# A hybrid decoder step on one core: the first two weight groups in four column pieces, and a new order in the head and ahead of the output projection

## The reference, cut to what matters

```python
def rmsnorm(x, g):
    y = xf * lax.rsqrt(jnp.mean(xf * xf, axis=-1, keepdims=True) + EPS)
    return (y * g).astype(x.dtype)
...
(gq, gk, gv, glr, gg, pv, pg, fq, fk, fv, ff, fg) = jnp.split(rmsnorm(h, pre) @ wi, SPLIT_IDX, axis=-1)
g = log_sigmoid(glr @ w_up + b_gate) / GLA_GATE_NORM     # GLA's gates, from 16 columns of wi
logf = log_sigmoid(ff + bf)                              # FoX's gates, from 6 columns of wi
...
y = jnp.concatenate([o_gla * silu(gg), o_pool * silu(pg), o_fox * silu(fg)], axis=-1) @ wo
return h + rmsnorm(y, post)
```

## Time and profile before

| | us |
|---|---|
| median of 3 runs | 697.47 (697.28 to 698.56) |
| the profiled execution | 697.7 |
| its span, first to last instruction | 696.1 |
| PE busy in it | 654.0 (94%) |
| DVE, ACT, POOL busy | 392.2, 261.3, 139.9 |

### The profile page before, as it was taken

How to read it: one execution, slowest core, us unless ns; L and a number is a source line. 1 busy time by engine, 2 the same in 40 slices (tenths; PEclk the granted TensorE clock), 3 DMA queues, 4 the chain that set the end, 5 groups by cost and what they waited for, 6 DMA issues and landing times.

```text
span 696.1 us, 13072 instructions
## 1 busy us (share of the span) xinstructions
PE 654.0 (94%) x5104; PEld 560.0 (80%) x5104; DVE 392.2 (56%) x706; ACT 261.3 (38%) x479; POOL 139.9 (20%) x161
## 2 busy tenths in 40 slices
PE   2899999999999999999999989998999887999996
PEld 2789999899999889999999965766667655688884
DVE  4833935763454415159999967335443468554543
ACT  6627334112111155221212063745564657232321
POOL 4035111211110011223312040123222201112210
PEclk9899999999999999999999999999999999999998
DMA  8411203041011031344120282557666523123132
GB/s 245 129 37 33 61 1 76 17 105 32 1 32 32 5 84 67 93 138 142 31 61 1 77 257 87 159 168 218 183 212 177 188 109 106 27 81 120 62 121 91
DMA packets 60759, 67.29 MB, mean 97 GB/s; under 512 B 15188, under 2 KB 50907, under 8 KB 60697
## 3 DMA queue, kind: packets, MB, share of 16 engines
q1 hardware_dynamic: 55529, 51.37, 25.2%
q0 software_dynamic: 5168, 15.08, 7.2%
HBM read 57.71 MB, written 8.68 MB: 95 GB/s over the span
## 4 chain that ended last, share of the span: by engine, by line
PE 80%; DVE 8%; ACT 4%; issue 3%; SPq 3%; DMA 1%; DVEq 0%; ACTq 0%
PE PS L1770 13%; PE PS L1771 13%; PE PS L1772 13%; PE PS L1698 4%; PE PS L1699 4%; PE PS L1700 4%; PE PS L2059 3%; PE PS L2041 3%; PE PS L1994 3%; PE PS L2016 2%; PE PS L1959 2%; PE PS L1946 2%; DVE rows_odd L1577 2%; DMA wr<-in_w_in_dram 1%; DVE YF L1456 1%
## 5 line engine op out<-in xcount | busy, mean ns | idle before, releaser
L1770 PE MATMUL PS<-xh,wh 128*128 128x368 f32 x576 | 196.1, 340 | 0.6 <-DVE RA L1396 0.3
L1771 PE MATMUL PS<-xl,wh 128*128 128x368 f32 x576 | 190.2, 330 | 0.0
L1772 PE MATMUL PS<-xh,wl 128*128 128x368 f32 x576 | 189.8, 329 | 0.0
L588 POOL TENSOR_TENSOR wl<-wr,wh 128x1024 fp32r<-128x1024 f32 x24 | 61.5, 2562 | 293.6 <-ACT wh L949 293.4
L1770 PEld LDWEIGHTS PS<-xh,wh 128*128 128x128 f32 x576 | 108.2, 188 | 4.7 <-issue 2.2
L1771 PEld LDWEIGHTS PS<-xl,wh 128*128 128x128 f32 x576 | 108.2, 188 | 0.9
L1772 PEld LDWEIGHTS PS<-xh,wl 128*128 128x128 f32 x576 | 108.2, 188 | 0.0
L1265 DVE TENSOR_TENSOR wr<-wr,small 128x1024 f32<-128x1024 f32 (+1 forms) x26 | 37.1, 1428 | 44.8 <-DMA wr<-in_w_in_dram 44.7
L1436 DVE RECIPROCAL RA<-RA 128x1104 f32<-128x1104 f32 x8 | 56.4, 7054 | 0.3
L1698 PE MATMUL PS<-woh,yh 128*128 128x512 f32 x128 | 50.5, 395 | 0.2 <-DVE zout L1616 0.2
L1700 PE MATMUL PS<-woh,yl 128*128 128x512 f32 x128 | 50.2, 392 | 0.0
(11 more groups left out here) (313 smaller groups left out, 1109.3 us busy)
## 6 DMA issues: line engine op xcount, KB each, us to landing
wr<-in_w_in_dram SPq DMA_DIRECT2D x24, 512.0 KB, 3.9
kpage<-in_cache_fox_k_dram SPq DMA_DIRECT2D x64, 192.0 KB, 2.6
RA<-in_cache_fox_v_dram POOLq DMA_DIRECT2D x32, 192.0 KB, 3.6
pagesB<-in_cache_fox_v_dram POOLq DMA_DIRECT2D x32, 192.0 KB, 3.7
YF<-in_x_prompt_dram SPq DMA_DIRECT2D x8, 512.0 KB, 7.0
xres<-in_x_prompt_dram SPq DMA_DIRECT2D x8, 512.0 KB, 3.9
out_y_p_dram<-zout SPq DMA_DIRECT2D x16, 256.0 KB, 2.1
wo_raw_a<-in_w_out_dram SPq DMA_DIRECT2D x6, 512.0 KB, 4.8
```

The source lines that it names most:

```text
L588: eng.tensor_tensor(low, wr[:, c % 2, :, 0:m], wh[:, c % 2, :, 0:m].bitcast(F32), ALU.subtract).then_inc(wlo_done, 1)
L1770: pe.matmul(out, high, xh[:, k, cols], start=(k == 0), stop=False)
L1771: pe.matmul(out, high, xl[:, k, cols], start=False, stop=False)
L1772: ins = pe.matmul(out, low, xh[:, k, cols], start=False, stop=(k == KT - 1))
```

## The change

Head. (1) `norm_pre` is loaded as 8 rows of 128 values in front of all other loads, turned by PE and copied to `gpre` by VectorE. (2) Group 1 is loaded ahead of the third prompt tile, group 0 behind it. (3) Both are scaled by GpSimd, group 1 first and in two halves; ScalarE copies group 1 in two halves. (4) Tiles 4, 6 and 8 are scaled by GpSimd, tiles 6 and 8 squared by VectorE. (5) Groups 0 and 1 are made in four column pieces of 272, 256, 256 and 320, by the rows of tiles 0 to 2, 3 and 4, 5 and 6, 7 and 8; group 1 comes first. The first piece takes the low part of the weights last. (6) VectorE scales group 2 behind all rows. Tail. (7) Quarter (2, 2) takes all blocks of the next quarter in its first pair of turns. (8) `TAIL` is rewritten: W 3 and W 4 ahead of the exponentials, fewer X in a row, and the sample's product behind the last turn.

```diff
+FIRST_COLS = [slice(0, NMETA + 2 * P), slice(NMETA + 2 * P, NMETA + 4 * P), slice(NMETA + 4 * P, NMETA + 6 * P),
+              slice(NMETA + 6 * P, NT)]
+FIRST_ROWS = [3, 5, 7, 9]
+SCALED_DVE, SCALED_POOL = [0, 1, 2, 3, 5, 7], [4, 6, 8]
+SQUARED_ACT, SQUARED_DVE = [0, 1, 2, 3, 4, 5, 7], [6, 8]
...
-        rooms = max(1, len(units) - 1 - after)
+        rooms = 2 if (p, q) == (2, 2) else max(1, len(units) - 1 - after)
...
+            order += BEHIND_TURNS.get(units[first], [])
             order += [("V", unit) for unit in behind]
...
-TAIL = {(2, 2, 0): [("W", 0), ("W", 1)], (2, 2, 1): [("W", 2)],
-        (2, 2, 2): [("X", 0), ("X", 1), ("W", 3)], (2, 2, 3): [("X", 2), ("X", 3), ("W", 4)],
-        (2, 3, 0): [("X", 4), ("W", 5), ("Y", FIRST)], (2, 3, 1): [("X", 5)], (2, 3, 2): [("W", 6)],
-        (2, 3, 3): [("W", 7), ("S", SAMPLE), ("X", 6), ("X", 7)], (2, 3, 4): [("E", SAMPLE)]}
+TAIL = {(2, 2, 0): [("W", 0), ("W", 1), ("W", 2)], (2, 2, 1): [("W", 3), ("W", 4)], (2, 2, 3): [("X", 0), ("X", 1)],
+        (2, 3, 1): [("X", 2), ("X", 3), ("W", 5), ("W", 6), ("Y", FIRST)], (2, 3, 3): [("X", 4), ("X", 5), ("W", 7)],
+        (2, 3, 4): [("E", SAMPLE)]}
+BEHIND_TURNS = {(2, 3, 4): [("S", SAMPLE), ("X", 6), ("X", 7)]}
...
+            for ks, done in ((slice(0, 4), wg_half), (slice(4, 8), wg_done)) if c == 1 else ((slice(0, KT), wg_done),):
+                w = wr[:, c % 2, ks, 0:m]
+                eng.tensor_tensor(w, w, gpre[:, ks, None].to_broadcast([P, ks.stop - ks.start, m]), ALU.mult
+                                  ).then_inc(done, 1)
...
+            sp.dma_start(gpre_rows, a["norm_pre"][0].rearrange("(k p) -> k p", p=P)).then_inc(d_gpre, 16)
             for i, t in enumerate(XORDER):
                 load_x(t)
-                if i == 1:
-                    with nc.allow_non_contiguous_dma(reason="one value per partition"):
-                        sp.dma_start(gpre[:, :], a["norm_pre"][0].rearrange("(k p) -> p k", p=P)).then_inc(d_gpre, 16)
+                if i == 2:
+                    load_w(1)
                 if i == 3:
                     load_w(0)
-                if i == 4:
-                    load_w(1)
...
+            w_scale(g, 1)
+            w_scale(g, 0)
+            for i in SCALED_POOL:
+                t = XORDER[i]
+                g.wait_ge(refined, SCALED_POOL.index(i) + 1)
+                g.tensor_scalar(xrows[:, t, :], xrows[:, t, :], rstd[:, t:t + 1], refine[:, t:t + 1],
+                                ALU.mult, ALU.mult).then_inc(xs_pool, 1)
             link(g.memset(pool_w[:, :, :], 0.0))
...
             x_squares(0)
             x_roots(0, 1)
-            for i in range(1, 9, 2):
...
+            x_squares(1)
+            x_roots(1, 1)
+            x_squares(2)
+            x_roots(2, 1)
+            x_high(0)
+            x_high(1)
+            act.wait_ge(wg_half, 1)
+            act.activation(wh[:, 1, 0:4, :], wr[:, 1, 0:4, :], ACT.Copy).then_inc(whi_half, 1)
+            x_high(2)
+            w_high(1)
+            w_high(0)
+            x_squares(3)
+            x_squares(4)
+            x_roots(3, 2)
+            x_squares(5)
+            x_high(3)
+            x_high(4)
+            x_roots(5, 2)
+            lf_high(0)
+            x_squares(7)
+            x_high(5)
+            x_roots(7, 2)
+            x_high(6)
+            lf_high(1)
             x_high(7)
-            lf_high(1)
             x_high(8)
+            lf_high(2)
...
             x_scale(0)
-            for i in range(9):
...
+            x_scale(1)
+            x_scale(2)
+            x_low(0)
+            x_low(1)
+            x_low(2)
+            w_low(dve, 1)
+            w_low(dve, 0)
+            x_scale(3)
+            x_squares(6)
+            x_low(3)
+            x_low(4)
+            x_scale(5)
+            lf_rest(0)
+            x_squares(8)
+            x_low(5)
+            x_scale(7)
+            x_low(6)
+            lf_rest(1)
+            x_low(7)
+            x_low(8)
+            lf_rest(2)
+            w_scale(dve, 2)
...
+                for i in range(3):
+                    x_transposes(i)
+                first_chunk(0)
+                low_rank(0)
+                x_transposes(3)
+                x_transposes(4)
+                first_chunk(1)
+                x_transposes(5)
+                x_transposes(6)
+                low_rank(1)
+                first_chunk(2, 7)
+                x_transposes(8)
+                low_rank(2)
+                low_rank(3)
+                first_chunk(3)
```

More of the change, by code:

```diff
@@ L920, in x_roots @@
                 m = n_of(t)
-                act.wait_ge(sq_done, i + n_)
+                if n_ == 2 and i + 1 in SQUARED_DVE:
+                    act.wait_ge(sq_done, SQUARED_ACT.index(i) + 1)
+                    act.wait_ge(sqv_done, SQUARED_DVE.index(i + 1) + 1)
+                else:
+                    act.wait_ge(sq_done, SQUARED_ACT.index(i + n_ - 1) + 1)
                 act.activation(refine[0:m, t:t + n_], ssq[0:m, t:t + n_], ACT.Identity, bias=eps[0:m, :], scale=1.0 / D)
@@ L1384, in store @@
                 if c == C_LF:
-                    lf_rest(2)
+                    lf_rest(3)
                 elif C_GV <= c < C_GV + 3:
                     dve.wait_ge(in_full, c + 1)
-                    dve.tensor_copy(thirds(Y[:, c - C_GV, :]), src).then_inc(done, 1)
+                    if c == 1:
+                        for n_, cols in enumerate(FIRST_COLS):
+                            ins = dve.tensor_copy(Y[:, 0, cols], first_out(n_))
+                        ins.then_inc(done, 1)
+                    else:
+                        dve.tensor_copy(thirds(Y[:, c - C_GV, :]), src).then_inc(done, 1)
                 elif c == C_GKA:
@@ L1716, in low_rank @@
             def low_rank(t):
-                cols = slice(TH * t, TH * t + TH)
+                cols = FIRST_COLS[t]
+                if t == 2:
+                    pe.wait_ge(lf_low, 1)
+                elif t == 0:
+                    pe.wait_ge(whi_done, scaled_at(0))
+                    pe.wait_ge(wlo_done, scaled_at(0))
+                pe.wait_ge(xlo_done, 2 * FIRST_ROWS[t])
                 for k in range(KT):
-                    both = (PS[0:64, 0, 0:TH], wh[:, 0, k, 0:64], xh[:, k, cols])
-                    rest = (PS[0:32, 0, 0:TH], wh[:, 0, k, 0:32], xl[:, k, cols])
+                    both = (low_out(t), wh[:, 0, k, 0:64], xh[:, k, cols])
+                    rest = (low_out(t, 32), wh[:, 0, k, 0:32], xl[:, k, cols])
                     if k:
@@ new lines, in low_rank, with first_chunk @@
+                ins.then_inc(in_full if t == 3 else lf_full, 1)
+            def first_chunk(t, rows_between=None):
+                cols, out = FIRST_COLS[t], first_out(t)
+                if t == 3:
+                    pe.wait_ge(lf_low, 2)
+                pe.wait_ge(xhi_done, 2 * FIRST_ROWS[t])
+                for k in range(KT):
+                    if t == 0 and k == 0:
+                        pe.wait_ge(whi_half, 1)
+                    elif t == 0 and k == 4:
+                        pe.wait_ge(whi_done, scaled_at(1))
+                    pe.matmul(out, wh[:, 1, k, :], xh[:, k, cols], start=(k == 0), stop=False)
+                    if t:
+                        pe.matmul(out, wl[:, 1, k, :], xh[:, k, cols], start=False, stop=False)
+                if rows_between is not None:
+                    x_transposes(rows_between)
+                pe.wait_ge(xlo_done, 2 * FIRST_ROWS[t])
+                for k in range(KT):
+                    ins = pe.matmul(out, wh[:, 1, k, :], xl[:, k, cols], start=False, stop=(t > 0 and k == KT - 1))
+                if t == 0:
+                    pe.wait_ge(wlo_done, scaled_at(1))
+                    for k in range(KT):
+                        ins = pe.matmul(out, wl[:, 1, k, :], xh[:, k, cols], start=False, stop=(k == KT - 1))
+                if t == 3:
+                    ins.then_inc(in_full, 1)
@@ new lines, in first_chunks @@
+            def first_chunks():
+                pe.wait_ge(d_gpre, 16)
+                pe.transpose(PS[:, 5, 0:KT], gpre_rows, ident[0:KT, 0:KT]).then_inc(gpre_full, 1)
+                for i in range(3):
[13 more added lines that the diff above has]
+                first_chunk(3)
@@ L1931, in side @@
                 ins.then_inc(ring_full, 1)
-            for i in range(5):
-                x_transposes(i)
             first_chunks()
```

143 lines of the change are left out of this document (59 added, 84 removed).

## The result

The changed kernel takes 693.59 us (median of 5 runs, 691.65 to 694.74) against 697.83 before, a ratio of 0.9943 (95% interval 0.9926 to 0.9959). The forecast was 691.8 with 688.6 to 694.9: faster, as forecast, and 1.8 us less so than its likeliest value. The profiled execution took 691.88 us (span 690.3), where the prediction's sum, 697.7 - 3.3 - 2.4, gave 692.0. So two questions stand: whether the sum was right term by term, and why the median lies above it.

What follows compares the result with a forecast made beforehand. TensorE was taken as nearly always busy, with time to win before its first product and in 5.3 us idle ahead of the output projection. 697.7 - 3.3 (head) - 2.4 (tail) = 692.0; median forecast 691.8, range 688.6 to 694.9.

Steps and rivals of the forecast that it cites:

- The pitch: Head, products of groups 0 and 1: 0.126, 0.119, 0.119 and 0.147 us for pieces of 272, 256, 256 and 320 columns.
- the rival of the weight load: Head: weight loads of 0.19 us set the product pitch, group 1 costs 6.0 us more; 697.5, no change (chance 0.05).
- First product: Head: TensorE's first product starts at 15.8 us, bounds 14.4 and 17.5, against 23.05 before.
- The added 0.8 us for VectorE beside GpSimd: Head, before the first product: VectorE's scaling slowed by GpSimd's scaling of group 1; 0.8 us, bounds 0 and 2.0.
- Loss (1): Head: first 16 products at the low clock, 0.23 us each in place of 0.126; 1.7 us lost, bounds 0 and 3.4.
- The rival's mechanism: Head: PE's gaps let the clock fall again, 3.4 us lost twice, head gain about 0; 695.3 (chance 0.09).
- Loss (2): Head: ScalarE's copies of rows 3 and 4 end after PE is free; 0.8 us lost, bounds 0 and 1.5.
- Loss (3): Head: PE waits for rows scaled by GpSimd; 0.8 us lost at row 6, taking 1.8 us a scaling, bounds 1.0 and 4.8.
- p: Head: time of one GpSimd scaling of row 4, 6 or 8, taken as 1.8 us.
- The slower rival: Head: GpSimd becomes the bound; gain gone and 0.2% more from 4.7 us a scaling, 701.4 at 5.5 (chance 0.04).
- Loss (4): End of the head, ahead of `project_in(2)`: group 2's scaling and splits outlast PE's products; 0.8 us lost, bounds 0 and 1.5.
- The tail: Ahead of the output projection: shorter waits for exponentials, `PT` and first output product; 2.4 us won, bounds 1.0 and 2.8.

Runs made afterwards that it cites:

- e4_filled: Changed kernel plus 22 transposes of the identity on PE, ahead of and between the first rows; median 693.73 us (6 runs), ratio 0.9947.
- e6: Changed kernel with VectorE's squares of row 8 moved right behind its squares of row 6; single run, 694.35 us.
- e10: Changed kernel with W 3 and W 4 moved behind both exponentials in the tail; single run, 692.67 us.
- e11: Changed kernel with the old line for `rooms`, so block (2, 7, 2) stands behind the second pair of turns again; single run, 696.22 us.
- e1: Changed kernel's head with the plan and TAIL of the kernel before; median 694.83 us (12 runs), ratio 0.9973.
- e5: Changed kernel with rows 4, 6 and 8 scaled by VectorE instead of GpSimd; single run, 692.8 us.
- e7: Changed kernel with VectorE's scaling of group 2 moved ahead of the remainders of row 7; single run, 692.78 us.
- e12: Changed kernel with remainders X 0 to X 3 in a row again, ahead of VectorE's copy of turn (2, 3, 1); single run, 693.19 us.
- e3_again: Changed kernel run again with no edit; median 694.46 us (8 runs, 691.74 to 697.48), ratio 0.9953.

## Why the prediction was right, step by step

**The pitch.** 0.118 us at 256 columns and 0.124 at 272 against 0.119 and 0.126 from the line through two other widths: the loads set nothing, and the rival of the weight load is gone.

**First product.** 15.35 against 15.8. The added 0.8 us for VectorE beside GpSimd did not occur: VectorE had scaled row 2 by 12.1, and GpSimd began at 12.04, because group 1 landed at 12.0 and not at 10.8. A late load took a collision away: luck, which made up for a path from the scaling to the product that took 3.2 us and not 3.0.

**Loss (1), clock:** the sixteen products took 3.8 us (15.35 to 19.14), 0.24 each, and the clock rose at 19.34, as put. `e4_filled` shows its worth as 0.4 us (0.7 from the first product on), not 1.7: it was mis-sized because it stood in the sum as if nothing waited behind it. Nor is it a fixed loss: with the same transposes ahead of the first product the clock rose at 14.3 to 15.7 in `e6`, `e10` and `e11`, before any product, and at 18.9 to 20.9 in the changed kernel's two traces, `e1`, `e5`, `e7` and `e12`; what decides it is not shown. The rival's mechanism, a clock that PE's gaps make fall again, occurred once: in `e11` it fell at 25.9, behind waits of 0.94 and 0.74 at row 4 and the second piece, and `project_in(2)` came at 46.59.

**Loss (2):** 0.84 against 0.8. **Loss (3):** 0.96 against 0.8, but for another reason: p was put at 1.8 and is 1.74 where no squares meet it, 2.79 and 3.13 at rows 4 and 6. The size is luck: with 1.73 at row 6 (`e6`) the wait was 0.30. The slower rival (p over 4.7) stayed far off. The prediction's estimate of 1.0 to 1.7 us from the Trainium skill (GPSIMD Engine Reference, 3.1 Elementwise) ends just below the 1.74, and says nothing of the 3.13. **Loss (4):** 0.54 against 0.8, of which 0.3 is again GpSimd beside VectorE (`e7`). The head won 3.08 us against 3.3.

**The middle.** The prediction left it alone; it gave 0.48 us, by the code packet. The step that failed is "what lies between them the change leaves alone": the change made TensorE's program longer (160 products of groups 0 and 1 in place of 120 and one transpose more, each with its weight load: 82 instructions), and that moved the packet.

**The tail.** The output projection starts 5.83 us earlier, 3.56 of it in hand since group 10: 2.27 from the tail against 2.4. Piece by piece: 0.67 left of 1.90 at the exponentials (0.8 forecast), 1.16 gone, 0.21 gone, 0.16 new at the sample's product (0.1 to 0.3). The splits ahead are worth 0.9 us, the earlier block 0.3, the shorter run of remainders about 1.6, each with the others in place; they add up to 2.8 and not to 2.27; no run undoes two of them at once, so how they overlap is not shown.

**The median.** 3.08 + 0.48 + 2.27 = 5.8 us is the difference of the two profiled executions, 697.7 and 691.88; the medians differ by 4.2 and, in the second set, 2.9. I set the one profiled execution equal to the median, but 697.7 is 1.6 above the lowest of its kernel on that chip (1.95 above the one run on the other) and 691.88 only 0.2 above that of the changed one. Of the 13 runs of the changed kernel 7 are over 2 us above its lowest, of the 31 of the two shared sets of the kernel before 8; the one such run with a profile lost 4.6 us to the clock in the middle. For the others the record has the mean granted clock alone, and it parts them: of the changed kernel the 5 runs at 0.998 or more took 691.65 to 692.89, the 8 at 0.996 or less 693.59 to 697.48; of the kernel before the 14 at 0.997 or more took 696.10 to 697.44, the 17 at 0.994 or less 696.93 to 700.07, with all 8 that are over 2 us above the lowest. Between the runs with the higher clock the medians are 696.9 and 691.9, 5.0 us apart. So the median lies above the sum by a term that the prediction did not have, stretches at the lower clock in 8 of the 13 runs (where they lie is shown for one); `e3_again`, with a median of 694.46, is only 0.4 inside the range. Whether the falls have become more frequent, and by what, stays open: the counts are too small, the traces show the same work at the same places with and without a fall, and no run here moved that work.

## What to carry to other kernels

Losses on one engine add only if nothing else is nearly late: before pricing a slow stretch in full, look how long each following operand has been ready. Where an engine gets work to relieve another, see which of the other's instructions will run beside it, and keep squares and two-input work away from the one that is waited for. And compare kernels by several runs and by the marks of their traces: a single profiled execution can stand 1.6 us from the lowest of its kernel before anything has been changed.

## What the runs showed of the hardware that was not expected

A 16 KB packet of code that meets a DMA issue on SyncE can lengthen it from 0.44 to 1.49 us, and all that SyncE issues behind it is late; 84 instructions more on TensorE moved it away. Not every meeting does so: in the kernel before six issues from 519.26 on took 2.12 us in all, 0.35 each, with a packet of code at 520.4 beside them. Waits that are already met cost TensorE's queue something: 84 instructions of them put the first transposes 5.1 us later. Transposes of the identity raised the clock at 7.6 us, with no product run (`e4_filled`). VectorE's squares (1.21 us) stretched a GpSimd scaling that had started before them, from 1.73 to 3.13 us, and were not stretched themselves. And the clock can fall to 1.2 GHz in the middle of the kernel while PE is recorded as busy without a gap (6.00 of 6.00 us, `e3_again`).
